# Three fused blocks on one core: two output tiles per input tile behind four normalizations, and sums of squares kept as rows

## What is computed

```
x = first_block(x)    # mixer, layer_norm, cross attention, layer_norm (ln2), conv-GLU FFN, layer_norm (ln3)
x = second_block(x)   # rms_norm (norm_mix), mixer, rms_norm (norm_ffn), product-key experts ("peer"), rms_norm (norm_final)
x = third_block(x, c) # rms_norm * (1+scale) + shift from w_ada @ silu(c); mixer; rms_norm (g_norm2) likewise; MLP; rms_norm
layer_norm(x) = (x - mean(x)) * rsqrt(mean((x-mean)^2) + eps) * g + b
rms_norm(x)   = x * rsqrt(mean(x^2) + eps) * g
```

## Time and profile before

| | us |
|---|---|
| median of three runs | 4124.14 |
| the profiled execution | 4120.71 |
| its span, first to last instruction | 4118.9 |
| PE busy | 3681.9 (89%) |
| DVE busy | 2343.7 (57%) |
| ACT busy | 1485.5 (36%) |
| POOL busy | 1236.9 (30%) |

### The profile page before, as it was taken

One profiled execution on the slowest core, in us unless ns is written; L12 is line 12 of the kernel. 1 busy time (PEld: TensorE's weight loads), 2 busy tenths in 40 slices (PEclk: granted clock), 3 DMA queues, 4 the chain that ended last, 5 costly groups with the idle time before them and its releaser, 6 DMA issues. The chain is left out here.

```text
span 4118.9 us, 39706 instructions
## 1 busy us (share of the span) xinstructions
PE 3681.9 (89%) x14504; PEld 2462.0 (60%) x14504; DVE 2343.7 (57%) x4183; ACT 1485.5 (36%) x3057; POOL 1236.9 (30%) x844
## 2 busy tenths in 40 slices
PE   8888898999999999799777777777789998999999
PEld 6755586788788778443232232232257666677887
DVE  3673353677925373467777777777641763355361
ACT  1133244443232453144444444444431554333221
POOL 0012252344410014133333333333321222243443
PEclk9999999999989999899999999999999999999999
DMA  3211131224612222499999999999941211122222
GB/s 119 77 41 67 57 132 52 72 92 174 271 51 103 88 91 101 168 415 421 421 416 421 421 407 421 421 405 421 421 165 63 77 52 57 62 82 82 103 92 82
DMA packets 113966, 791.04 MB, mean 192 GB/s; under 512 B 13360, under 2 KB 13680, under 8 KB 22128
## 3 DMA queue, kind: packets, MB, share of 16 engines
q0 software_dynamic: 73728, 536.90, 31.5%
q1 hardware_dynamic: 40048, 251.63, 17.1%
HBM read 786.38 MB, written 2.10 MB: 191 GB/s over the span
## 5 line engine op out<-in xcount | busy, mean ns | idle before, releaser
L2852 PE MATMUL bank<-arena 128*128 128x512 f32 x1984 | 965.8, 614 | 264.7 <-ACT arena L2900 244.8
L965 PE MATMUL bank<-rounded,weights_hi 128*128 128x512 f32 (+1 forms) x2248 | 877.2, 390 | 43.1 <-DVE rounded L1049 16.0
L915 POOL TENSOR_TENSOR weights_lo<-weight_ring,weights_hi 128x1024 fp32r<-128x1024 f32 (+3 forms) x245 | 566.6, 2313 | 1109.0 <-ACT weights_hi L987 1108.8
L966 PE MATMUL bank<-rounded,weights_hi 128*128 128x512 f32 (+1 forms) x2248 | 868.3, 386 | 0.0
L967 PE MATMUL bank<-rounded,weights_lo 128*128 128x512 f32 (+1 forms) x2248 | 868.3, 386 | 0.0
L2852 PEld LDWEIGHTS bank<-arena 128*128 128x128 f32 x1984 | 348.3, 191 | 848.9 <-issue 828.3
L2944 DVE SCALAR_TENSOR_TENSOR arena<-arena,bank 128x1024 f32<-128x1024 f32 x512 | 624.6, 1221 | 341.2 <-DMA arena<-in_experts,arena 338.4
L2931 POOL DMA_INDIRECT arena<-in_experts,arena x512 | 480.7, 939 | 877.0 <-PE bank L2852 711.1
L987 ACT ACTIVATE weights_hi<-weight_ring 128x1024 fp32r<-128x1024 f32 (+3 forms) x297 | 299.1, 1007 | 947.8 <-PE bank L967 940.9
L965 PEld LDWEIGHTS bank<-rounded,weights_hi 128*128 128x128 f32 x2248 | 424.2, 189 | 147.9 <-issue 19.4
L967 PEld LDWEIGHTS bank<-rounded,weights_lo 128*128 128x128 f32 x2248 | 424.1, 189 | 85.9
(11 more groups left out here) (437 smaller groups left out, 4293.7 us busy)
## 6 DMA issues: line engine op xcount, KB each, us to landing
arena<-in_w_ada SPq DMA_DIRECT2D x48, 512.0 KB, 8.1
weight_ring<-in_w_up SPq DMA_DIRECT2D x22, 1024.0 KB, 5.0
weight_ring<-in_w_down SPq DMA_DIRECT2D x8, 1408.0 KB, 6.1
weight_ring<-in_w_ga SPq DMA_DIRECT2D x8, 1024.0 KB, 4.9
weight_ring<-in_w_gb SPq DMA_DIRECT2D x8, 1024.0 KB, 4.9
weight_ring<-in_w_q SPq DMA_DIRECT2D x8, 1024.0 KB, 9.1
arena<-in_experts,arena POOLq DMA_INDIRECT x512, 15.2
weight_ring<-in_w_mlp1a SPq DMA_DIRECT2D x8, 1024.0 KB, 4.8
```

Source lines behind the costliest of these rows:

```text
L915: eng.tensor_tensor(lo, raw(m), hi.bitcast(F32), ALU.subtract).then_inc(s.lo_made.sem, 1)
L965: pe.matmul(bank(n)[:, 0:p.n], hi[:, k - k0, :], x.hi(k), start=first, stop=False)
L966: pe.matmul(bank(n)[:, 0:p.n], hi[:, k - k0, :], x.lo(k), start=False, stop=False)
L2852: mm = pe.matmul(total[:, half * T:(half + 1) * T], diag[:, j, :], rows[:, j, D + half * T:D + (half + 1) * T], start=i % SLOTS == 0, stop ...
```

## The change

1. **Two tiles at once.** Where a layer has a seam with no plan of its own and a third place (`two_at_once`: w_up, w2_ax, w3_nq, w3_mlp1a, all four of which get a `more_room`), PE takes the first two output tiles together: six products for each input tile k. ACT's part of the seam makes the first three weights' high parts (`first_weights`) ahead of the inputs' high parts.
2. **Sums as rows.** In ln2, ln3, norm_mix and NormTwice, one product a tile sums the squares: ones (one column; two columns of weights in NormTwice) are the weights, the 128x512 squares run through, and the sums are a row of 512. The root is taken of the row (NormTwice copies its rows first), four small products turn it into 128x4, and the reciprocal reads that from PSUM. Two `warm` products ahead of the spread are left out there.
3. **The last modulation group** (6 of the 48) moves on DVE from ahead of w_down's last evacuation to behind the tiles of w2_ax.
4. **The first two weights of w3_nq** are split at the end of the peer stage (`split_ahead`), on ACT and POOL, and the table for the root is loaded there.

```diff
@@ -861,6 +862,7 @@
...
+        p.two_at_once = bool(p.seam and p.more_room and not p.seam.pe_plan)
...
@@ -877,6 +879,9 @@
...
+    for q in parts:
+        if q.two_at_once:
+            q.seam.third_unit = q.start
...
@@ -945,9 +950,13 @@
...
+                if p.two_at_once and t == 1:
+                    continue
+                at_once = tiles[n:n + 2] if p.two_at_once and t == 0 else tiles[n:n + 1]
+                for i in range(n, n + len(at_once)):
+                    if i >= BANKS:
+                        before, t_before, _ = tiles[i - BANKS]
+                        pe.wait_ge(counter[before.by].sem, before.first_taken + t_before + 1)
...
@@ -956,16 +965,20 @@
...
                 for c, (k0, k1) in enumerate(p.chunks):
-                    hi, lo = halves(m + c)
-                    pe.wait_ge(s.lo_made.sem, split0 + nth[m + c] + 1)
+                    for _, _, unit in at_once:
+                        pe.wait_ge(s.lo_made.sem, split0 + nth[unit + c] + 1)
                     for k in range(k0, k1):
                         first, last = k == 0, k == p.kt - 1
                         if p.fresh and t == 0:
                             pe.wait_ge(s.act_lo.sem, s.act_lo.at(p.round0 + k + 1))
-                        pe.matmul(bank(n)[:, 0:p.n], hi[:, k - k0, :], x.hi(k), start=first, stop=False)
-                        pe.matmul(bank(n)[:, 0:p.n], hi[:, k - k0, :], x.lo(k), start=False, stop=False)
-                        mm = pe.matmul(bank(n)[:, 0:p.n], lo[:, k - k0, :], x.hi(k), start=False, stop=last)
-                    mm.then_inc(s.units_done.sem, 1)
+                        for i, (_, _, unit) in enumerate(at_once):
+                            hi, lo = halves(unit + c)
+                            out = bank(n + i)[:, 0:p.n]
+                            pe.matmul(out, hi[:, k - k0, :], x.hi(k), start=first, stop=False)
+                            pe.matmul(out, hi[:, k - k0, :], x.lo(k), start=False, stop=False)
+                            mm = pe.matmul(out, lo[:, k - k0, :], x.hi(k), start=False, stop=last)
+                            if k == k1 - 1:
+                                mm.then_inc(s.units_done.sem, 1)
...
@@ -976,10 +989,13 @@
...
+            rounded_weights = set(range(ahead))
+
             def high(m):
                 p, slab, u, c, _ = units[m]
-                if m < ahead or not p.split:
+                if m in rounded_weights or not p.split:
                     return
+                rounded_weights.add(m)
...
@@ -1013,7 +1029,15 @@
...
+            def first_weights(seam):
+                def high_parts():
+                    if seam.third_unit is not None:
+                        at = tiles[seam.third_unit][2]
+                        for m in range(at, at + UNITS + 1):
+                            high(m)
+                return high_parts
...
@@ -1151,7 +1177,16 @@
             pe.wait_ge(self.squared_too.sem, self.squared_too.at(t // 2 + 1))
         else:
             pe.wait_ge(self.squared.sem, self.squared.at(t // 2 + 1))
-        self.columns(pe, self.slots[t % 2], t == 0, t == DT - 1).then_inc(self.used.sem, 1)
+        if self.by_rows:
+            pe.matmul(self.s.ps[7][0:1, :], self.s.ones[:, 0:1], self.slots[t % 2], start=t == 0, stop=t == DT - 1).then_inc(self.used.sem, 1)
+        else:
+            self.columns(pe, self.slots[t % 2], t == 0, t == DT - 1).then_inc(self.used.sem, 1)
+
+    def turn_row(self, pe):
+        pe.wait_ge(self.root.sem, self.root.at(1))
+        for j in range(TT):
+            mm = pe.matmul(self.s.ps[5][:, j:j + 1], self.row[:, j * P:(j + 1) * P], self.s.ones[0:1, 0:1], start=True, stop=True)
+        mm.then_inc(self.turned.sem, 1)
 
     def column_of_total(self, pe):
         pe.wait_ge(self.used.sem, self.used.at(DT - 1))
...
@@ -1165,11 +1200,18 @@
...
-        act.activation(self.col, self.s.ps[7][:, 0:TT], ACT.Sqrt, bias=self.s.eps[self.eps], scale=1.0 / D).then_inc(self.root.sem, 1)
+        if self.by_rows:
+            act.activation(self.row, self.s.ps[7][0:1, :], ACT.Sqrt, bias=self.s.eps[self.eps][0:1, :], scale=1.0 / D).then_inc(self.root.sem, 1)
+        else:
...
     def turn_over(self, dve):
-        dve.wait_ge(self.root.sem, self.root.at(1))
-        dve.reciprocal(self.col, self.col).then_inc(self.root.sem, 1)
+        if self.by_rows:
+            dve.wait_ge(self.turned.sem, self.turned.at(1))
+            dve.reciprocal(self.col, self.s.ps[5][:, 0:TT]).then_inc(self.root.sem, 1)
+        else:
+            dve.wait_ge(self.root.sem, self.root.at(1))
+            dve.reciprocal(self.col, self.col).then_inc(self.root.sem, 1)
...
@@ -1233,18 +1275,22 @@
...
                 yield
-        self.warm(pe, 2)
-        x.spreads(pe)
-        self.warm(pe, 6)
+        self.spread(pe, x)
         yield
         if y:
             for t in range(DT):
                 y.column_of_square(pe, t)
                 yield
+            self.spread(pe, y)
+            yield
+
+    def spread(self, pe, x):
+        if x.by_rows:
+            x.turn_row(pe)
+        else:
             self.warm(pe, 2)
-            y.spreads(pe)
-            self.warm(pe, 6)
-            yield
+        x.spreads(pe)
+        self.warm(pe, 6)
 
     def high(self, act, k):
         x = self.last
...
@@ -1288,6 +1334,7 @@
...
+        first_weights()
...
@@ -1338,12 +1387,13 @@
...
         for t in range(DT):
             pe.wait_ge(self.squared.sem, self.squared.at(t + 1))
-            for j in range(TT):
-                mm = pe.matmul(sums[:, j, :], self.slots[t % 2][:, j * P:(j + 1) * P], self.weights[:, t, :], start=t == 0 and j == 0, stop=t == DT - 1, skip_group_check=True)
-            mm.then_inc(self.used.sem, 1)
+            pe.matmul(s.ps[7][0:2, :], self.weights[:, t, :], self.slots[t % 2], start=t == 0, stop=t == DT - 1).then_inc(self.used.sem, 1)
+        pe.wait_ge(self.turned.sem, self.turned.at(1))
+        for j in range(TT):
+            mm = pe.matmul(self.sums[:, j, :], self.rows[:, j * P:(j + 1) * P], s.eye[0:2, 0:2], start=True, stop=True)
+        mm.then_inc(self.turned.sem, 1)
...
@@ -1360,25 +1410,25 @@
...
-        act.activation(s.small[:, 240:241], s.eps[self.eps], ACT.Sqrt)
...
         act.wait_ge(self.used.sem, self.used.at(DT))
+        act.activation(self.rows, s.ps[7][0:2, :], ACT.Copy).then_inc(self.turned.sem, 1)
+        act.wait_ge(self.turned.sem, self.turned.at(2))
...
+        first_weights()
...
@@ -2314,6 +2365,14 @@
...
+    def modulate_before(dve, step, t):
+        if t < DT - 1:
+            modulate(dve, step, t)
+
+    def modulate_last(dve, step, t):
+        if t < ADA_GROUP:
+            modulate(dve, step, DT - 1, t)
...
@@ -2322,15 +2381,15 @@
...
+    ln2 = RowNorm(s, s.x, s.x, True, 0, s.col("ln2_g"), s.col("ln2_b"), tile(0), (tile(1), tile(2)), by_rows=True)
+    ln3 = RowNorm(s, s.x, s.x, True, 0, s.col("ln3_g"), s.col("ln3_b"), tile(72), (tile(73), tile(72)), by_rows=True)
+    norm_mix = RowNorm(s, s.x, s.n, False, 1, s.col("norm_mix"), None, None, (tile(73), tile(72)), by_rows=True)
...
+        part("w_up", Split(lambda k: s.x[:, k, :], DT, s.rounded(53), s.rounded(61)), take, after=convolve, side=silu, seam=Seam(s, "w_xo", ln2, keep=True), more_room=room_for_weights(s, 44)),
...
+             evac_before=modulate_before, act_at={2: silu_row}, made_by=lambda k: (min(2 * k + 2, 2 * FF_TILES - 1), gated_ready, gated_ready.at(k + 1))),
+        part("w2_ax", s.n_split, store(lambda t: s.ax[:, t, :]), seam=Seam(s, "w_down", ln3, norm_mix), more_room=room_for_weights(s, 40), after=modulate_last),
...
@@ -2917,6 +2977,8 @@
...
+            next_high(act)
+            act.activation(s.small[:, 240:241], s.eps[1], ACT.Sqrt)
...
@@ -2930,6 +2992,7 @@
...
+            next_low(pool)
...
@@ -3052,7 +3115,7 @@
...
+        part("w3_nq", h, store(lambda t: s.nq[:, t, :], scale=NSA_DH ** -0.5), seam=norms, more_room=room_for_weights(s, 40)),
...
@@ -3871,7 +3934,7 @@
...
+        parts.append(part("w3_mlp1" + name, h_split, evac, by="dve", **({"seam": Seam(s, "w3_out", normed), "more_room": room_for_weights(s, 56)} if name == "a" else {})))
```

More of the change, by code:

```diff
@@ L1014, in behind @@
                         seam.keep_behind(act, n - start)
-            running = [(seam.on_act(act), seam, p, last, start) for seam, p, last, start in seams]
+            def first_weights(seam):
[5 more added lines that the diff above has]
+                return high_parts
+            running = [(seam.on_act(act, first_weights(seam)), seam, p, last, start) for seam, p, last, start in seams]
             high(0)
@@ L1087, with __init__ @@
 class RowNorm:
-    def __init__(self, s, src, dst, center, eps, gain, bias, total, squares, on_dve=False):
+    def __init__(self, s, src, dst, center, eps, gain, bias, total, squares, on_dve=False, by_rows=False):
+        self.by_rows, self.row = by_rows, squares[0][0:1, :]
```

(23 more changed lines are left out.)

21 lines of the change are left out of this document (5 added, 16 removed).

## The result

The changed kernel took **4089.52 us** (median; 4088.22 to 4090.55), the kernel before 4123.39 beside it: ratio **0.9916**, 95% interval 0.9900 to 0.9932. The forecast was 4086 within 4073 to 4104. The profiled execution took 4089.48, with a span of 4087.7. The page opens with the busy times, to be set beside the earlier trace rows: PE works 27 us less (ln2, ln3, norm_mix and NormTwice have no passes of one or two columns any more, and fewer warm products), and keeps its 89%.

What follows compares the result with a forecast made beforehand. PE, busy 89% of the span, was taken as the bound, with four seams to shorten. Terms summed to -40.2, or -36.5 with clock losses; from 4120.7 that gave 4084.2, with half the median's 3.4 4086, range 4073 to 4104.

Steps and rivals of the forecast that it cites:

- Part 1: ln2 ahead of w_up: sums as rows, root with a turn, and two tiles at once, together -8.45 us.
- (a): Part 1: sums as rows, -4.9; Part 2: centring sooner after w_down, -5.5; Part 3: squares start at block's beginning, -2.25.
- (b): Part 1: root to first scale, +0.55; Part 2: centre to first root, -3.7; Part 3: first square to root, -4.8.
- (c): Part 1: first two tiles together, -4.1; Part 2: root to scale, +0.55; Part 3: row copy and turn, +1.9.
- Part 2: ln3 and norm_mix ahead of w2_ax: modulation group moved, sums as rows, two tiles at once, together -15.9 us.
- Part 3: NormTwice ahead of w3_nq: weights and table prepared in the peer stage, rows, two tiles at once, together -12.35 us.
- Part 4: Ahead of w3_mlp1a: sums stay columns, only two tiles at once counts, less 0.6 for POOL's low part: -3.5 us.
- The clock: PE nearly idle during root and turn; clock expected lost at two of the four passages, +1.85 us each.
- Third weights late: At each seam the third tile's weights come 3.5 us late, losing 14 of the pairs' 17: 4099; chance 0.07.
- Rows that don't hold the clock: In the norms, one column of weights fails to hold PE's clock: 4117 to 4120, no measurable change; chance 0.05.
- The change not doing what it says: At some seam the pair runs at DVE's pace, second weights missing: gives back 4 to 6, 4091, inside the range.
- w_up bound by DVE: In w_up, POOL's moved operation holds a second DVE operation per tile, 6.7 per tile: +50, 4134; chance 0.04.

Runs made afterwards that it cites:

- columns again: The changed kernel with the sums of squares of ln2, ln3 and norm_mix as passes of one column again: 4101.28 us.
- one at a time: The changed kernel with each first tile made before the second after the four norms, third place for weights kept: 4104.02 us.
- modulation back: The changed kernel with the last modulation group back between w_down's last tiles on DVE, ahead of ln3: 4093.80 us.
- early split: The changed kernel with w3_nq's first weights split earlier in the peer stage, POOL's low parts in among the gathers: 4083.71 us.

## Why the prediction was right, and where it was not

Time, direction and range came out; the forecast was 3.5 us too low. The steps by their own numbers:

- **Part 1, ln2: right.** -8.45 expected, -8.3 measured. (a) The rows took 7.28 (7.2). (b) Root to scale 3.25 (3.3). (c) The pair 10.98 (10.9). With columns again, the seam is 4.2 longer, as 4.9 less 0.55 says.
- **Part 2, ln3 and norm_mix: right.** -15.9 expected, -16.1 measured. (a) Centring 2.83 after the last product (2.83), where it was 8.53 after 1119.31 and not 8.32: the term is 5.7 rather than 5.5. (b) Centre to root 8.73 (8.6). (d) Scale to the second root 11.71 (11.7): the queues followed held. (f) 11.0 (10.9), from 14.5 (the sum read 14.4). Of (a), the price if the cover were gone was too small: the run that took it away shows 7.5, since the longer idle time of PE takes the clock with it.
- **Part 3, NormTwice: the step that failed is (a).** -12.35 was expected, -4.7 came. The prediction put POOL's low parts beside DVE's end and charged "0.15 for the block's end". That sentence was right about POOL and DVE (3015.77 and 3015.84) and wrong about the end of the stage: a 7.5 us pause, in which POOL's queue is at its DRAIN, and whose longer counterpart had been hidden behind 22 us of an idle POOL. DVE's last addition to the first square went from 2.8 to 7.5, +4.6 rather than -2.25: 6.9 of the 7.6 missing. The rest is (b), 10.84 rather than 9.8 from first square to the copy, as the clock was 0.50 for four rows rather than two or three. But that is this one execution: with the same pause and instructions (b) took 9.26, 9.29 and 9.63 in three of the experiments (columns again, one at a time, modulation back), and 9.45 in the early split without the pause. So 9.8 was right for (b), and the pause accounts for the miss. (c) 1.72 (1.9), (d) 3.00 (3.1) and (e), the pair at 10.98, were right. What the trace of before did show was an idle POOL; the step moved work into it, as the last instruction of a queue, and no bound was put on what the stage's end waits for behind that queue. The trace had a sign of it too, for who asked by the stage's line: the DRAIN that ended 17.9 us behind the last gather. The bound of 2.4 ("if POOL held DVE's last two operations") was for another mechanism.
- **Part 4, w3_mlp1a: right.** -3.5 expected, -3.8 measured. POOL's operation overlapped DVE's first low part by 0.4 only, which cost 0.2 instead of 0.6.
- **The clock.** 3.7 was charged for clock lost at two of the four passages. ln2 kept it; at ln3 it fell at 1129, when the turn and the spread were over, and root to scale took 3.25 all the same; NormTwice lost it during the pause (and in the kernel before, at the same place, without one). So the 3.7 wasn't spent, and that is why the forecast is only 3.5 off rather than 7: two errors of opposite sign. That the forecast came so near is in this part luck. With the pause's 6.9 and the slower rows' 1.0 added back, the seams give 40.8, against 40.2 in the prediction's sum before the clock.

**The rivals.** Third weights late: none; at every seam the `room` product follows the pair without a wait. Rows that don't hold the clock: refuted by the windows under them, 1.00. The change not doing what it says: refuted by four pairs of 11.0. **w_up bound by DVE** went the other way. Windows of w_up's steady stretch, the kernel before, then the changed one:

```profile
775.00:1000.00 225.00, 225.00 (x994) 186.30 (x993) 178.80 (x166) 94.94 (x131) 98.61 (x42) 1.00 0.30 102
...
775.00:1000.00 225.00, 225.00 (x994) 186.33 (x993) 154.39 (x167) 94.50 (x130) 111.05 (x41) 1.00 0.28 97
```

The prediction had a second DVE operation held per tile. DVE instead fell from 178.80 to 154.39 while POOL rose from 98.61 to 111.05. The groups by line tell where: the first step of the convolution (x41) fell from 2158 ns on average to 614, the last (x21) rose from 752 to 2386. Splitting a tile ahead has moved POOL's operation from the head of DVE's convolution to its end. PE had 225.00 of 225 in both, so it is worth nothing here. The rule that the prediction took from the Trainium skill (SBUF — State Buffer, Who interferes with whom) fits where an overlap is seen: the low part of 2.89 above began with POOL's operation and ended 0.55 after POOL did. The operation that was held before, the first step of the convolution, reads one tile and constants, which the sentence as the prediction has it doesn't cover; it is held all the same (in the changed kernel 2.46 at 767.40, beside POOL's 2.71 from 766.87, against 0.49 at 765.26).

## What to carry to other kernels

When work is moved into an idle engine, ask not only whether it is done in time but what the end of the stage waits for behind that queue: on POOL, with gathers in the same queue, leave 7.5 us between its last computing instruction and the stage's end, and 18 between its last gather and that end, or put the work among the gathers. Where no engine has an operation at a stage's end, ask the profile for the stage's own line. Small reductions over the partitions were cheaper as rows of 512 than as passes of one column, even with a turn added, because the rows kept the clock. Where DVE feeds PE at half its pace, two output tiles at once cost nothing but a third place for weights, and brought 3.5 to 4.0 us at each seam.

## What the runs showed of the hardware that was not expected

- Behind a stage in which POOL had issued gathers, the next one began 7.5 us after POOL's last instruction in the changed kernel and 7.54 in the kernel before with a 0.20 us operation added; it took 0.3 where the queue held no gathers. POOL's DRAIN fills that time: it ended 7.27 and 7.25 behind a last computing operation, 17.9 behind a last gather, and 0.07 behind the last operation of a stage without gathers. Whether the number of gathers matters was not tried.
- A PE that is busy throughout can run at 0.50 (passes of one column) or at 1.00 (rows of 512), at the same busy share. A few warm products of 128 columns, put where PE waits, kept 1.00 through a whole norm.
- The same POOL operation beside the same DVE code cost DVE 24 us less in 225 of w_up, by standing at another place in it; POOL itself was busy 12 longer.
